# Expert-gather opening respaced, one weight half moved to VectorE, and query weight panels issued from two engines, in a two-layer encoder kernel

## The reference

```python
def peer(x, w_q, sub_keys, u_tab, v_tab):
    q = (xt @ w_q).reshape(n_tok, PEER_HEADS, 2, D_QHALF)
    sc = jnp.einsum("thcd,hckd->thck", q, sub_keys)
    top_s, top_i = lax.top_k(sc, PEER_TOPK)
    ...
    best_s, best_j = lax.top_k(cand_s, PEER_TOPK)
    experts = jnp.take_along_axis(cand_e, best_j, axis=-1)
    gates = jax.nn.softmax(best_s, axis=-1)
    ...
    h = jnp.einsum("thkd,td->thk", u_tab[experts], x)
    return jnp.einsum("thk,thkd->td", gates * gelu(h), v_tab[experts])
```

## Time and profile before

| | us |
|---|---|
| median of 3 runs (lowest, highest) | 3249.26 (3247.75, 3254.29) |
| the profiled execution | 3249.95 |
| its span, first to last instruction | 3248.2 |
| TensorE, VectorE, ScalarE, GpSimd busy | 2846.5, 2491.4, 904.5, 1718.7 |
| moved by DMA | 1108.33 MB, 341 GB/s on average |
| query product of layer 0, layer 1 | about 342 to 450, 2001 to 2110 |
| U stage after it, until V gathers begin | about 450 to 1046, 2110 to 2705 |

### The profile page before, as it was taken

The page is one execution under the profiler, slowest core; times in us unless marked ns, Lnnn a source line. Parts: engine busy times, 40 slices in busy tenths (PEclk is TensorE's granted clock), DMA queues, the critical chain, the costliest instruction groups (busy, mean ns, idle before and its releaser), DMA issues.

```text
span 3248.2 us, 45298 instructions
## 1 busy us (share of the span) xinstructions
PE 2846.5 (88%) x15483; PEld 2197.7 (68%) x15483; DVE 2491.4 (77%) x3648; ACT 904.5 (28%) x1391; POOL 1718.7 (53%) x1446
## 2 busy tenths in 40 slices
PE   8999986777777999999999999966768778999998
PEld 8988976666777644444798978966667776444443
DVE  7995799999998866666534645899999998766666
ACT  4345432113433600000234534322124335100000
POOL 7770776666676644444200003676757776544443
PEclk9999988778988999999999999988879889999999
DMA  8655689999999999999755434899999999999998
GB/s 219 166 164 181 221 345 422 421 422 389 421 422 422 334 409 408 410 409 409 265 211 192 142 138 161 305 419 422 422 397 414 422 422 358 388 409 408 409 407 342
DMA packets 326933, 1108.33 MB, mean 341 GB/s; under 512 B 22228, under 2 KB 153876, under 8 KB 253716
## 3 DMA queue, kind: packets, MB, share of 16 engines
q0 software_dynamic: 147456, 805.37, 61.1%
q1 hardware_dynamic: 179348, 301.26, 26.5%
HBM read 1104.45 MB, written 2.10 MB: 341 GB/s over the span
## 4 chain that ended last, share of the span: by engine, by line
DMA 37%; PE 25%; DVE 19%; issue 9%; POOL 6%; ACT 2%; POOLq 0%; DVEq 0%; ACTq 0%
DMA ring<-in_peer_u,index_now 14%; DMA work<-in_peer_v,index_add 12%; DVE ring L2027 8%; DMA more_add<-in_peer_v,index_add 7%; PE ps L844 5%; PE ps L887 5%; POOL ring L671 4%; PE ps L961 3%; DVE ps L2099 3%; PE ps L898 2%; DMA more_add<-in_peer_v,index_v 2%; PE ps L970 2%; DMA ring<-in_peer_w_q 1%; PE ps L1153 1%; PE ps L1215 1%
## 5 line engine op out<-in xcount | busy, mean ns | idle before, releaser
L671 POOL DMA_INDIRECT ring<-in_peer_u,index_now x464 | 745.3, 1606 | 359.0 <-issue 129.3
L2027 DVE SCALAR_TENSOR_TENSOR ring<-ring,x_tok 128x2048 f32<-128x2048 f32 x360 | 813.4, 2288 | 64.8 <-DMA ring<-in_peer_u,index_now 59.1
L1228 PE MATMUL ps<-all_v,mix 128*128 128x512 f32 x1984 | 851.8, 592 | 0.0
L1228 PEld LDWEIGHTS ps<-all_v,mix 128*128 128x128 f32 x1984 | 377.1, 190 | 474.3 <-issue 474.3
L1181 PE MATMUL ps<-x_dot,work 128*128 128x128 f32 x3840 | 517.8, 299 | 126.3 <-DVE ps L2034 75.3
L1181 PEld LDWEIGHTS ps<-x_dot,work 128*128 128x128 f32 x3840 | 495.9, 213 | 156.0 <-issue 78.1
L2099 DVE SCALAR_TENSOR_TENSOR ps<-work,coef,ps 128x1024 f32<-128x1024 f32 x326 | 419.2, 1287 | 224.6 <-DMA work<-in_peer_v,index_add 195.1
L1573 ACT ACTIVATE work<-ps 128x1024 f32<-128x1024 f32 x240 | 236.2, 1022 | 573.4 <-PE ps L1175 572.8
L1798 DVE TENSOR_TENSOR w_lo<-ring,w_hi 128x2048 fp32r<-128x2048 f32 x85 | 194.8, 2291 | 255.8 <-ACT w_hi L1381 237.9
L796 POOL DMA_INDIRECT work<-in_peer_v,index_add x256 | 241.5, 943 | 263.4 <-DVE ps L2099 211.8
L1175 PE MATMUL ps<-ident,ring 128*128 128x128 f32 x1920 | 272.4, 303 | 88.0 <-DMA ring<-in_peer_u,index_now 58.8
(11 more groups left out here) (268 smaller groups left out, 4614.0 us busy)
## 6 DMA issues: line engine op xcount, KB each, us to landing
all_v<-in_peer_v SPq DMA_DIRECT2D x248, 512.0 KB, 6.8
ring<-in_conv_w_in SPq DMA_DIRECT2D x32, 1024.0 KB, 9.1
ring<-in_peer_w_q SPq DMA_DIRECT2D x16, 2048.0 KB, 11.3
ring<-in_attn_w_kv SPq DMA_DIRECT2D x16, 2048.0 KB, 8.0
ring<-in_conv_w_out SPq DMA_DIRECT2D x8, 2048.0 KB, 7.8
ring<-in_attn_w_q SPq DMA_DIRECT2D x8, 2048.0 KB, 8.4
ring<-in_attn_w_o SPq DMA_DIRECT2D x8, 2048.0 KB, 7.7
ring<-in_peer_u,index_now POOLq DMA_INDIRECT x464, 13.2
```

The lines of the kernel that those rows point to most:

```text
L671: pool.indirect_dma_start(tile, None, u_tab, bass.IndirectOffsetOnAxis(ap=index_now[:, half, s:s + 1], axis=0)).then_inc(landed_in, 16)
L1228: mm = pe.matmul(ps[:, dense_bank(tb, q), :], mix[tb][:, row, :], tile[:, q * 512 - HALF:(q + 1) * 512 - HALF], start=False, stop=True, sk ...
L2027: dve.scalar_tensor_tensor(out=tile, in0=tile, scalar=1.0, in1=x_tok[:, tb, :], op0=ALU.mult, op1=ALU.mult, accum_out=coef[:, tb, slot]).t ...
```

## The change

Three edits, in both layers alike.

- Half 6 is split by VectorE (after the expert numbers of head 0) instead of GpSimd.
- GpSimd's early gathers are spaced otherwise between its splits: 3, 1, 2, 3, 3, 4 around halves 7, 9, 11, 13, 15 instead of 2, 1, 3, 2, 3, 3, 2 around halves 6, 7, 9, 11, 13, 15. VectorE's early dots are re-placed between splits and routing, and the pairs of heads 2 and 3 are routed after dot 8 instead of dot 12.
- Panels 2 to 7 are loaded by two DMAs of 1 MB: SyncE the first 8 of 16 row blocks, ScalarE the last 8. ScalarE issues its part of panel `p` after it has copied half `2p - 4`, and first waits for the split of half `2p - 3`, as SyncE does. Both parts increment the panel's semaphore, and `landed` counts them.

```diff
+        def loaded_by_two(n):
+            return any(first + 2 <= n < first + PANELS for first in P_WQ)
         def landed(n):
-            return (n - P_OUT) // 2 + 1
+            return sum(2 if loaded_by_two(m) else 1 for m in range(n, P_OUT - 1, -2))
...
                     to, src = panel_chan(local % 2), by_columns(w)[:, :, p * 256:p * 256 + 256]
+                if loaded_by_two(n):
+                    to, src = to[:, 0:KC // 2, :], src[:, 0:KC // 2, :]
                 sp.dma_start(to, src).then_inc(panel[local % 2], 16)
...
                 pool.wait_ge(route[layer], part_done(0, 0))
-                gather_early(0, 2)
-                next_half(6)
-                gather_early(2, 3)
+                gather_early(0, 3)
                 next_half(7)
-                gather_early(3, 6)
+                gather_early(3, ROOMS)
                 next_half(9)
-                gather_early(6, 8)
+                gather_early(ROOMS, 6)
                 next_half(11)
-                gather_early(8, 11)
+                gather_early(6, 9)
                 next_half(13)
-                gather_early(11, 14)
+                gather_early(9, 12)
                 next_half(HALVES - 1)
-                gather_early(14, EARLY)
+                gather_early(12, EARLY)
...
+                def load_second(p):
+                    n = P_WQ[layer] + p
+                    act.wait_ge(w_split, 2 * (n - P_OUT - 1))
+                    rows = peer_w_q[layer].rearrange("(c p) n -> p c n", p=P)
+                    act.dma_start(panel_chan((n - P_OUT) % 2)[:, KC // 2:KC, :],
+                                  rows[:, KC // 2:KC, p * 256:p * 256 + 256]).then_inc(panel[(n - P_OUT) % 2], 16)
...
                     act.activation(q_now[:, m % 8, :], ps[:, query_bank(m), 0:S], ACT.Copy).then_inc(chunk_taken, 1)
+                    if m % 2 == 0 and m // 2 + 2 < PANELS:
+                        load_second(m // 2 + 2)
...
                 part_keys(0, 0, 1)
+                next_half(6)
                 route_keys(layer, 0, 1, 2)
                 route_pairs(layer, 0, 1, 2)
-                early_dots(0, 2)
-                next_half(8)
-                early_dots(2, 3)
+                early_dots(0, 1)
                 part_numbers(layer, 0, 1, 2)
                 part_key(layer, 0, 1, 2, 0)
-                early_dots(3, 4)
-                next_half(10)
+                early_dots(1, 2)
+                next_half(8)
                 part_key(layer, 0, 1, 2, 1)
                 part_index(layer, 0, 1, 2)
-                early_dots(4, 7)
+                early_dots(2, 4)
+                next_half(10)
+                early_dots(4, 5)
+                route_keys(layer, 0, 2, 3)
+                early_dots(5, 6)
                 next_half(12)
-                route_keys(layer, 0, 2, 3)
-                early_dots(7, 10)
+                early_dots(6, 8)
+                route_keys(layer, 0, 3, 4)
                 next_half(14)
-                route_keys(layer, 0, 3, 4)
-                early_dots(10, 13)
+                early_dots(8, 9)
                 route_pairs(layer, 0, 2, 4)
-                early_dots(13, EARLY)
+                early_dots(9, EARLY)
```

## The result

The changed kernel takes 3261.76 us (median of 7 runs, 3252.85 to 3264.03) against 3249.26 us (now also of 7 runs): ratio 1.0033, 95% interval 1.0022 to 1.0043. That is slower by more than the 0.2% that can be told from no change; 3242 was forecast, with 3252 as the upper end. The profiled execution took 3252.85 us (span 3251.1), the lowest of the seven.

The account below looks back on a forecast made before the run. Bound: the DMA-bound ring's start, set by the opening. VectorE's 60.0 us plus 6.7 of waits replace 71.1, 4.5 earlier; some 0.7 returns, called 4 us per layer, 8 in two: 3249.95 - 8 = 3242, range 3233 to 3252.

Parts of the forecast that it names:

- The bound: Opening before the DMA-bound ring: idle DMA time of 8.3 us in layer 0 is nearly all a better opening can win.
- All three arrive before or within 3 us of the time at which TensorE's halves allow the rounding: Panels 5, 6 and 7 land in about 9.5, 12 and 14.5 us, so ScalarE's and TensorE's waits for panel 5 go.
- The waits: VectorE waiting for early tiles: 1.8 us at dot 0, 3 at dot 4, 1.9 at dot 6, sum 6.7.
- the forecast's 60.0 of work: VectorE from first gather to dot 11 without waits: 54.5 us plus half 6 (2.2) and pair routing (3.3).
- I take nothing, since after the spread the panels are no longer last anywhere: Panel loads by two queues: gain between nothing and a panel landing as if alone in 8.0 us; costed at nothing.
- Rival C: ScalarE's parts, issued behind roundings, chain the panels; 5, 6, 7 each 3.3 us late, +5 per layer: 3260; chance 0.10.
- Rival A: Pair routing beside GpSimd's last split waits for its end, 2.9 us per layer; gain 1 us, 3248; chance 0.22.
- B: Early gathers land in 5.5 us, dots 0, 4 and 6 hardly wait; about 8 us gained per layer, 3234; chance 0.14.
- D: No change: the gathers, later by the spread, land as late as before; 3250; chance 0.10.
- Gathers 4 and 5 behind half 9: At dot 4 VectorE waits for GpSimd's split, then the gather: between 2.5 and 6 us, taken as 3.

Follow-up runs that it names:

- r8: Kernel before with half 6 split by VectorE alone, so the third early gather goes ahead of half 7; one queue: 3243.76 us, 0.9978.
- r2: Changed kernel without ScalarE's part: half 6 on VectorE and the new orders, every panel in one DMA from SyncE: 3253.10 us, 1.0002.
- r18: r8 with the fourth early gather, too, in front of half 7: 3255.48 us, 1.0007.
- r1: The changed kernel run again, unaltered: 3263.91 us, 1.0035 against the kernel before.
- r10: Changed kernel with both parts of each panel issued by SyncE, back to back in one queue: 3253.93 us, 1.0014.
- r3: Kernel before, orders kept, with panels 2 to 7 loaded by SyncE and ScalarE: 3249.27 us, 0.9995.
- r5: Changed kernel with the third early gather behind half 7 instead of in front of it: 3254.73 us, 1.0008.
- r6: r2 with the third early gather behind half 7 instead of in front of it: 3253.65 us, 1.0008.
- r11: r2 with SyncE issuing panels 3 to 7 only after ScalarE rounded the first half of the panel before: 3264.52 us, 1.0048.
- r15: r8 with gathers 4 and 5 moved behind half 9: 3247.49 us, 0.9994.
- r13: r2 with gathers 4 and 5 issued in front of half 9 instead of behind it: 3265.72 us, 1.0050.
- r7: Changed kernel with panel 4 in one DMA from SyncE, panels 2, 3, 5, 6 and 7 still in two parts: 3257.93 us, 1.0017.
- r16: r2 with GpSimd's gathers and splits ordered as in r8, VectorE's order as in the change: 3266.45 us, 1.0040.
- r17: r2 with VectorE's dots, halves and routing ordered as in r8, GpSimd's order as in the change: 3265.37 us, 1.0038.
- r4: Changed kernel with ScalarE issuing its part of a panel ahead of the rounding instead of behind it: 3267.07 us, 1.0046.

## Why the prediction was wrong

**The bound was right.** The opening's holes decide, the ring's rate doesn't change, and a shift of the ring's start reaches the end (from the first ring gather to the first gather of `peer_v`, layer 0 takes 596.3 us before and 596.6 after): r8's ring starts 3.1 and 4.0 us sooner and its time is 7.1 us less. GpSimd's 5 us split and the 4.9 us pair operation beside it went as forecast, and so did ScalarE's long wait for panel 5 and TensorE's gap in 400 to 410.

**"All three arrive before or within 3 us of the time at which TensorE's halves allow the rounding" failed on the panel it left out.** I counted tiles beside panels 5, 6 and 7. The third early gather, which goes at 382.56 before, in the last 5 us of panel 4, goes at 379.30 now, right among panel 4 and the two others. ScalarE waits 8.59 us for panel 4, where it waited 4.42, and 8.00 in r2. The crowd had moved to the panel in front, on which half 8, half 9 and gathers 4 and 5 hang. r18 shows the same with a fourth tile: 14.32 us. And the landings of the panels that I did count were too small: 9.5, 12 and 14.5 us for panels 5, 6 and 7, against 13.2, 13.3 and 17.0 in r2, which has the spread with one queue. My sum shared the full rate among a panel and the gathers issued beside it, and left out what was under way already: when panel 5 is issued in r2, panel 4 and two gathers have yet to land (4.9, 0.7 and 4.7 us later).

**The waits were mis-sized: 6.7 us forecast, 12.3 measured.** Gather 0 goes at 375.55 and dot 11 ends at 448.3, 72.8 us: the forecast's 60.0 of work, some 0.5 of other pieces, and waits of 0.64 (half 6), 2.08 (dot 0), 1.89 (half 8), 4.10 (dot 4), 1.20 and 0.61 (dots 6 and 7) and 1.81 (half 14). Dots 0, 4 and 6 are near the 1.8, 3 and 1.9 that I took; halves 6, 8 and 14, for which I took nothing, are 4.3 of the 5.6 us that were missing. So VectorE's work was added up rightly, and the panels still stand on its path. Together with the 60.0 this explains why the order alone gives nothing (r2), not why it is slower.

**"I take nothing, since after the spread the panels are no longer last anywhere" failed.** This is the costing of ScalarE's part, and the step that turned the sign: the term was put at nothing and measured 10 to 11 us in the new order (after and r1 against r2). ScalarE waits longest for panels 4, 6 and 7, in r2 as in the changed kernel, and a later landing of panel 4 then counts. That the issuer matters and not the cut is shown by r10 (both parts from SyncE, 3253.93). In the old order (r3) and with the third gather behind half 7 (r5 against r6) the second queue costs nothing.

Rival C had the sign and nearly the number (3260, measured 3261.76), and I gave it 0.10; but most of that is luck. What C feared exists (r11, SyncE made to wait for the roundings, 3264.52), and the chain of waits runs through ScalarE's parts. Yet C made panels 5, 6 and 7 late, 3.3 us each, and in the trace they take no more than 0.4 us longer than with one queue. The trace has the second issuer's cost at panel 4, whose part is issued behind no landing, and it is small there: the rings start 0.6 and 1.6 us later than r2's. That C's chain makes the level near 3262 is thus not shown. The Trainium skill (DMA: Bandwidth & Descriptors, section "Issuing engines are not separate DMA queues") says that spreading DMAs over engines saves issue time alone. The runs agree in so far as r3 gains nothing by it (0.9995). They don't agree that nothing else changes: panel 4 landed later with ScalarE as second issuer (18.8 and 18.5 us in r1, 17.2 and 16.8 in r10), and the measurement decides.

**Rival A was there, at half its size.** The pairs of heads 2 and 3 meet GpSimd's last split (434.85 to 439.97) and take 1.92 us for two operations that take 0.45 without it: 1.5 us, and not the 2.9 of waiting for the split's end. They start at 436.89, when 3.1 us of the split are left, and aren't held for all of that. The Trainium skill (SBUF - State Buffer, section "SBUF: two separate sides") has the loser block for a full instruction. The trace agrees if that instruction is one of the split's four (5.12 / 4 = 1.3 us), and not with A's reading, in which the whole split was one.

**Rivals B and D.** B needed gathers that land in 5.5 us; gathers 0 to 8 took 9.1 to 12.7 in the changed kernel. D, no change, is what the order did by itself (r2, ratio 1.0002).

**Gathers 4 and 5 behind half 9** were seen as a 3 us wait of dot 4 (measured 4.10), but not as a hole: 90 GB/s in 400 to 405. It is worth 4 to 5 us in r8's order (r15). In the new order, moving them back makes things worse (r13), so it can't be booked as that order's loss.

**Open.** Why most executions of the changed kernel are 9 us above its profiled one: r11's trace shows such a level with late panels 4 and 7, but whether the same happens inside the changed kernel no trace shows. A part may lie outside the openings: from the first gather of `peer_v` to layer 1's first query matmul, a stretch that no edit touches, the traces take 955.6 us (before) to 961.1 (r7). r7's rings start as early as r2's (108.0 and 108.1 us), and its median is still 4.8 us above r2's. So a difference of a few us between two single traces can't be booked to the opening alone. Open too is what each wait in the mixed orders (r13, r16, r17) is worth, and whether an order exists that spreads and keeps r8's gain; none was found.

## What to carry to other kernels

When a load is taken off one crowded transfer, count the company of the transfers before it as well, and follow which splits and gathers hang on each. Count the gathers issued right behind a load: here a panel of 2 MB took 8.0 us at best, and panel 4, loaded by SyncE in one DMA, 13 to 14 us with two, 16.4 to 17.1 with three and 23.0 with four. Try a second issuer by itself before it is costed at nothing, and let the engine that issues a load be one that doesn't wait for the load before it (r11). Lay the trace of a changed kernel beside that of its own parts, and not only beside the one before. Change one piece of a hand-written order at a time: here the smallest piece, half 6 on VectorE and with it the third gather ahead of half 7, gave 0.22%, and the full rewrite with the second queue lost 0.33%.

## What the hardware showed that I had not expected

Panels and gathers don't share evenly. Beside three gathers of 1.05 MB, which landed in 9.7, 11.1 and 11.9 us, the second megabyte of a panel took 16.5 us (20.2 in r4), while the first took 5.6. It is so whoever issues them: in r10 SyncE issued both ahead of the first gather, 0.41 us apart, and they took 5.5 and 16.8 us; the panel in one piece took 16.7 in r2.

```profile
L544 SPq DMA_DIRECT2D ring<-in_peer_w_q x1: 367/367/367, 374.4 to 374.4; - x1
...
DMA to landing us min/median/max: 16.7/16.7/16.7
```

A panel comes in rows of 1 KB (256 columns of 4 bytes), a tile in rows of 8 KB; in these traces the panel is in only when the three tiles are. Whether the size of the rows is the reason no run tried. The Trainium skill (DMA: Bandwidth & Descriptors, section "Queues, rings and completion order") has each DMA engine take turns between queues packet by packet; no run here shows the turns. A panel on two queues instead of one didn't land sooner, but later. A sum of bytes over bandwidth sees neither: 5.2 MB at 423 GB/s is 12.4 us, and the panel took 16.4 to 20.9.
